# Attention scores and dilated value products of two heads issued in turn into halves of the array, with the dilated mask added on VectorE

## The chip, the cores and the metric

The kernel runs on one core of one Trainium2 chip. The metric is the device time of one execution in microseconds (us), the median of several runs; lower is better.

## The reference

A two-layer encoder on 256 tokens of width 1024, in float32. Each layer is a sandwich-normed mixer and a gated MLP with a centred convolution. The mixer projects the normed input once and splits the result into gates and three kinds of attention:

```python
proj = jnp.einsum('bsd,dc->bsc', h, w_in[l])
gates, mla_in, dil_in, diff_in = jnp.split(proj, SPLITS, axis=-1)
o_mla = mla_mixer(...)        # 8 heads, keys 64 + 32 wide, values 64 wide
o_dil = dilated_mixer(...)    # 6 heads of 64, three groups: dilation 1, 4 and 16
o_diff = diff_mixer(...)      # 4 heads, each softmax(q0 k0) - lam * softmax(q1 k1), 64 wide; values 128 wide
merged = g_mla * (o_mla @ w_branch_mla[l]) + g_dil * (o_dil @ w_branch_dil[l]) + g_diff * (o_diff @ w_branch_diff[l])
x = x + rms_norm(merged @ w_out[l], attn_post_norm[l])
x = x + rms_norm(conv_gated_mlp(rms_norm(x, ...), w_up[l], ffn_conv[l], w_down[l]), ffn_post_norm[l])
```

In the dilated mixer, a query sees the keys of its own residue class that lie within a radius. The three groups' outputs are weighted by the softmax of their log-sum-exps, which is the same as one softmax over the scores of the three groups side by side.

## The kernel before, in words

Weights stream in 87 **pieces** a layer (`PIECES`, line 72). SyncE loads a piece into one of three buffers, ScalarE copies it to a rounded high part `w_hi` (line 617), VectorE subtracts to get the low part `w_lo` (line 906), and TensorE does three matmuls for each product (low by high, high by low, high by high: lines 1170 to 1172). A piece of four 512-column blocks is 24 such matmuls (two row tiles, four blocks, three passes).

The order of all engines is one hand-made list of steps (`plan_steps`, line 116), which each engine walks through in its own program. Step `w` uses a piece: TensorE multiplies it, while ScalarE and VectorE prepare the piece two further on. The attention steps lie between the `w` steps:

- `score i` (28 a layer): i 0 to 7 is latent attention, one query tile of two heads (contraction over 96 rows, line 1337). i 8 to 15 is differential attention, one of the two softmaxes of a head (contraction over 64 rows, either rows 0 to 63 or 64 to 127, line 1343). i 16 to 27 is dilated attention, one query tile of one head: a bf16 matmul of an identity by the mask (line 1348) writes the mask into the bank, then one product of 256 columns and two of 128 are added to it (lines 1349 and 1351; contraction over 64 rows). Odd and even i have their own PSUM banks (4 and 5) and their own slot of `probs`.
- The softmax of score i: VectorE takes the negated maximum (lines 931 and 934), ScalarE the exponential with its sum (lines 791 and 795), VectorE scales (lines 946 to 961).
- `tp i`: TensorE transposes the 128 by 512 probabilities in four parts (line 1416) into bank 6, the only one for it after the first ten; ScalarE copies them to `probsT` (lines 681 and 684), which has two slots. For i 8, 10, 12, 14 there is none.
- `pv g` (14 a layer): value products into bank 7. g 0 to 3 is a pair of latent heads, each into its own 64 output partitions (line 1367), head after head; g 4 to 7 is a differential head over the full array (line 1373); g 8 to 13 is one dilated head into 64 output partitions (lines 1380 and 1383). ScalarE and VectorE empty the bank (lines 803 to 805 and 967 to 975).
- `tq s`: transposes of queries and keys staged by ScalarE and turned by GpSimd's rotation (lines 1406 and 1409), into bank 6 as well; ScalarE empties. `td`: transposes of the differential outputs (line 1423).

A float32 product stands in the trace as two MATMUL records. A transpose is one record.

The order before, in the stretch of the dilated scores, is `score i, pv, w, tp i-1, score i+1, w, tp i, ...`: one `w` between two scores.

Of the kernel before, what the change touches and what calls it, by code (L numbers as in the profile page):

```python
# [16 lines left out]
P = 128  # L39
# [11 lines left out]
HD = 64  # L51
# [63 lines left out]

def plan_steps():
# [163 lines left out]
def build_trunk(nc, a, out):  # L280
    with ExitStack() as ctx:
# [15 lines left out]
        ident_b = sb("ident_b", [P, P], BF16)  # L297
# [9 lines left out]
        half = sb("half", [P, 1])  # L307
        head_squares = sb("head_squares", [P, SEQ])
# [4 lines left out]
        with ExitStack() as one:  # L313
# [13 lines left out]
            probsT = sb("probsT", [P, 2, 4, SEQ], scope=one)  # L327
# [37 lines left out]


# [120 lines left out]
        def _(pool):  # L487
# [11 lines left out]
            for h in range(2):  # L499
# [4 lines left out]
            nc.gpsimd.memset(ident_b[:], 0.0)  # L504
            nc.gpsimd.memset(mask[:], 0.0)
            pool.drain()
            nc.gpsimd.affine_select(out=ident_b[:], in_=ident_b[:], compare_op=ALU.not_equal, fill=1.0, base=0,
                                    pattern=[[-1, P]], channel_multiplier=1)
# [89 lines left out]
        def _(act):  # L598
# [55 lines left out]
            def empty_t(l, key):  # L654
# [20 lines left out]
                elif what == "tp":  # L675
                    g, qt = i // 2, i % 2
                    if g >= 2:

                        act.wait_ge(o_full, l * 14 + (g - 1))
                    if 8 <= i < 16:  # L680
                        nc.scalar.activation(probsT[:, g % 2, 0:2, :].rearrange("p k (t q) -> p t k q", t=2),
                                             T_BANK[:].rearrange("p (t k q) -> p t k q", t=2, k=2), ACT.Copy).then_inc(t_emptied, 1)
                    else:
                        nc.scalar.activation(probsT[:, g % 2, :, qt * P:qt * P + P], T_BANK[:].rearrange("p (b q) -> p b q", b=4),  # L684
                                             ACT.Copy).then_inc(t_emptied, 1)
# [59 lines left out]
            with act.Fori(0, DEPTH) as l:  # L745
                split_hi(l, 0)
                for step in STEPS:
# [31 lines left out]
                    elif what == "score":  # L779
                        i = step[1]  # L780
                        act.wait_ge(max_done, l * 28 + (i + 1))
                        if 10 <= i <= 16 and i % 2 == 0:

                            act.wait_ge(probs_ready, l * 28 + i)
                        elif i >= 2:

                            act.wait_ge(t_full, l * NTB + (T_OF[("tp", i - 2)] + 1))
                        b = i % 2
                        if i < 16:
                            for h in range(2):  # L790
                                last = nc.scalar.activation(probs[:, b, h * SEQ:(h + 1) * SEQ], S_BANK[b][:, h * SEQ:(h + 1) * SEQ], ACT.Exp,
                                                            bias=negmax[:, 2 * b + h:2 * b + h + 1],
                                                            accum_out=rowsum[:, 2 * b + h:2 * b + h + 1])
                        else:
                            last = nc.scalar.activation(probs[:, b, :], S_BANK[b][:], ACT.Exp, bias=negmax[:, 2 * b:2 * b + 1],
                                                        accum_out=rowsum[:, 2 * b:2 * b + 1])
                        last.then_inc(exp_done, 1)
                    elif what == "pv":
                        g = step[1]
                        if g < 4 or g >= 8:  # L800
                            act.wait_ge(o_full, l * 14 + (g + 1))
                            if g < 4:
                                nc.scalar.activation(mla_oT[:, g, 0, :], O_BANK[:, 0:SEQ], ACT.Copy).then_inc(o_hi, 1)
                            elif g % 2 == 1:
                                nc.scalar.activation(dil_oT[:, (g - 8) // 2, 0, :], O_BANK[:, 0:SEQ], ACT.Copy).then_inc(o_hi, 1)
# [36 lines left out]
        def _(dve):  # L842
# [84 lines left out]
            def negmax_of(l, i):  # L927
                b = i % 2
                dve.wait_ge(score_full, l * 28 + (i + 1))
                if i < 16:  # L930
                    V.tensor_reduce(negmax[:, 2 * b:2 * b + 2], S_BANK[b][:].rearrange("p (h k) -> p h k", h=2), AX.X, ALU.max,
                                    negate=True).then_inc(max_done, 1)
                else:
                    V.tensor_reduce(negmax[:, 2 * b:2 * b + 1], S_BANK[b][:], AX.X, ALU.max, negate=True).then_inc(max_done, 1)
# [29 lines left out]
            def empty_o(l, g):  # L964
# [3 lines left out]
                elif g < 8:  # L968
                    dve.wait_ge(o_full, l * 14 + (g + 1))
                    h = g - 4  # L970
                    V.tensor_copy(diff_o[:, :, h * P:(h + 1) * P], O_BANK[:, 0:SEQ].rearrange("p (t d) -> p t d", t=2)).then_inc(o_emptied, 1)
                elif g % 2 == 1:
                    pair = (g - 8) // 2
# [74 lines left out]
            with dve.Fori(0, DEPTH) as l:  # L1048
# [5 lines left out]
                for step in STEPS:  # L1054
# [40 lines left out]
                    elif what == "score":  # L1095
                        negmax_of(l, step[1])
                        normalise(l, step[1])
# [48 lines left out]
        def _(pe):  # L1146
# [54 lines left out]
            def use_piece(l, n):  # L1201
# [30 lines left out]
                if kind == "bmla" or kind == "bdil":  # L1232

                    pe.wait_ge(o_emptied, BASE + l * 11 + (4 if kind == "bmla" else 11))
# [30 lines left out]
            def turn(l, what):  # L1265
# [9 lines left out]
                if what == "merged":  # L1275
                    pe.wait_ge(o_emptied, BASE + l * 11 + 11)
# [49 lines left out]
            def scores(l, i):  # L1326
                if i in (0, 4, 8, 16):
                    wait_heads(l, i)
                b = S_BANK[i % 2]
                qt = i % 2  # L1330
                q = slice(qt * P, qt * P + P)
                if i >= 2:
                    pe.wait_ge(exp_done, l * 28 + (i - 1))
                if i < 8:
                    pair = i // 2
                    for h in range(2):
                        last = PE.matmul(b[:, h * SEQ:(h + 1) * SEQ], mla_qT[0:QK_M, 2 * pair + h, q], mla_kT[0:QK_M, 2 * pair + h, :], start=True, stop=True)
                elif i < 16:

                    head, m = i // 2 - 4, i % 2  # L1340
                    r = slice(64 * m, 64 * m + 64)
                    for t in range(NT):
                        last = PE.matmul(b[:, t * SEQ:(t + 1) * SEQ], diff_qT[r, head, t * P:(t + 1) * P], diff_kT[r, head, :], start=True, stop=True)
                else:
                    head = i // 2 - 8
                    pe.wait_ge(masks_ready, 1)
                    r = slice(64 * (head % 2), 64 * (head % 2) + 64)
                    PE.matmul(b[:], ident_b[:], mask[:, qt, :], start=True, stop=False, skip_group_check=True)
                    PE.matmul(b[:, 0:SEQ], dil_qT[r, head // 2, 0, q], dil_kT[r, head // 2, 0, :], start=False, stop=True, skip_group_check=True)
                    for g in (1, 2):  # L1350
                        last = PE.matmul(b[:, P + g * P:2 * P + g * P], dil_qT[r, head // 2, g, q], dil_kT[r, head // 2, g, q],
# [116 lines left out]
```

## Time and profile before

| | |
|---|---|
| median of 3 runs | 1103.39 us (1103.26 to 1105.31) |
| span of the profiled execution | 1100.7 us |
| TensorE busy | 1081.7 us, 98% |
| VectorE, ScalarE, GpSimd busy | 60%, 53%, 11% |
| granted TensorE clock, mean | 0.996 |
| HBM traffic | 154 GB/s over the span |

The span runs from the first to the last instruction of one profiled execution. The page of the profile gives no device time of its own for that execution, so the span is set beside the median of the runs, which is 2.7 us longer. Busy time of TensorE counts each matmul from its start to its modelled end, and matmuls overlap in the pipeline: the pace has to be read from start to start.

### The profile page before, as it was taken

How to read it: one execution, taken by the hardware profiler on the slowest of the kernel's cores; microseconds unless marked ns; L12 is line 12 of the kernel's file. 1: busy time of each engine (PE TensorE's matmuls, PEld its weight loads, DVE VectorE, ACT ScalarE, POOL GpSimd, SP SyncE). 2: the span in 40 equal slices, each digit the busy share in tenths (PEclk: the TensorE clock that was granted, in tenths of full speed). 3: DMA queues.
4: the chain of work that ended last, by engine and by line, in shares of the span. 5: the costliest groups of instructions: out<-in, count | busy, mean ns of one | idle time of the engine just before them, and what ended most of it. 6: DMA issues, size and time to landing. Idle time of an engine off the chain costs nothing.

```text
span 1100.7 us, 18061 instructions
## 1 busy us (share of the span) xinstructions
PE 1081.7 (98%) x6428; PEld 954.0 (87%) x6428; DVE 663.8 (60%) x842; ACT 585.6 (53%) x843; POOL 124.3 (11%) x237
## 2 busy tenths in 40 slices
PE   8999999999999999999999999999999999999997
PEld 8889889877778899999888898898877779999996
DVE  5535556555476777677664455655545767776765
ACT  5556655454435754555476566555544466455552
POOL 3252113100000000000014321221000000000000
PEclk9999999999999999999999999999999999999999
DMA  6654444533344455455355544364333445546541
GB/s 191 217 163 144 118 123 163 177 130 115 134 154 153 134 192 205 164 206 189 117 178 168 155 135 125 115 194 152 115 121 127 155 133 192 200 164 212 189 157 38
DMA packets 105665, 170.98 MB, mean 155 GB/s; under 512 B 3057, under 2 KB 72484, under 8 KB 105572
## 3 DMA queue, kind: packets, MB, share of 16 engines
q1 hardware_dynamic: 104564, 166.37, 46.2%
q10 hardware_dynamic: 864, 3.15, 1.0%
q8 instruction: 54, 0.88, 0.3%
q0 software_dynamic: 144, 0.26, 0.1%
q14 instruction: 39, 0.32, 0.1%
HBM read 168.72 MB, written 1.05 MB: 154 GB/s over the span
## 4 chain that ended last, share of the span: by engine, by line
issue 45%; PE 45%; POOL 3%; POOLq 3%; DVE 2%; ACT 1%; DVEq 1%; DMA 1%; SPq 0%; ACTq 0%
PE bank L1170 14%; PE bank L1172 14%; PE bank L1171 14%; POOLq L546 2%; POOL stage L547 1%; PE bank L1156 1%; POOLq L573 1%; DVE hT_lo L923 1%; POOL rope_b L545 1%; POOL small L590 1%; DMA par_rows<-in_ffn_conv_dram 1%; POOL rope_a L544 0%; POOL stage L548 0%; POOL roots L594 0%; PE bank L1299 0%
## 5 line engine op out<-in xcount | busy, mean ns | idle before, releaser
L906 DVE TENSOR_TENSOR w_lo<-w_raw,w_hi 128x2048 fp32r<-128x2048 f32 (+3 forms) x174 | 361.7, 2091 | 146.8 <-ACT w_hi L617 146.7
L617 ACT ACTIVATE w_hi<-w_raw 128x2048 fp32r<-128x2048 f32 (+3 forms) x174 | 302.7, 1753 | 35.0 <-PE bank L1172 29.1
L1170 PE MATMUL bank<-w_hi,hT_lo 128*128 128x512 f32 (+2 forms) x704 | 260.6, 370 | 1.8 <-DVE hT_lo L923 1.8
L1172 PE MATMUL bank<-w_hi,hT_hi 128*128 128x512 f32 (+2 forms) x704 | 254.4, 361 | 0.0
L1171 PE MATMUL bank<-w_lo,hT_hi 128*128 128x512 f32 (+2 forms) x704 | 253.9, 361 | 0.0
L1170 PE MATMUL bank<-hT_hi,w_lo 128*128 128x256 f32 x704 | 200.0, 284 | 3.4 <-DVE hT_lo L923 3.4
L1171 PE MATMUL bank<-hT_lo,w_hi 128*128 128x256 f32 x704 | 199.1, 283 | 0.0
L1172 PE MATMUL bank<-hT_hi,w_hi 128*128 128x256 f32 x704 | 199.0, 283 | 0.0
L1170 PEld LDWEIGHTS bank<-w_hi,hT_lo 128*128 128x128 f32 x704 | 132.2, 188 | 19.5 <-issue 2.7
L1172 PEld LDWEIGHTS bank<-w_hi,hT_hi 128*128 128x128 f32 x704 | 132.1, 188 | 14.2
L1171 PEld LDWEIGHTS bank<-w_lo,hT_hi 128*128 128x128 f32 x704 | 132.4, 188 | 12.9
L1170 PEld LDWEIGHTS bank<-hT_hi,w_lo 128*128 128x128 f32 x704 | 134.8, 192 | 6.0 <-DVE hT_lo L923 5.1
L1171 PEld LDWEIGHTS bank<-hT_lo,w_hi 128*128 128x128 f32 x704 | 134.9, 192 | 0.8
L1172 PEld LDWEIGHTS bank<-hT_hi,w_hi 128*128 128x128 f32 x704 | 134.9, 192 | 0.0
L822 ACT ACTIVATE conv_out<-bank,par 128x256 f32<-128x256 f32 x88 | 36.9, 471 | 125.5 <-PE bank L1172 125.5
L594 POOL TENSOR_TENSOR roots<-mean_squares,minus_half 128x1 f32<-128x1 f32 x12 | 6.5, 546 | 667.2 <-DVE mean_squares L1004 667.2
L1127 DVE SCALAR_TENSOR_TENSOR conv_out<-bank,par,conv_out 128x255 f32<-128x255 f32 x88 | 38.4, 478 | 54.4 <-ACT conv_out L822 54.4
L1170 PE MATMUL bank<-w_hi,g_lo 128*128 128x512 f32 x176 | 69.6, 396 | 0.8 <-DVE g_lo L1141 0.8
L1172 PE MATMUL bank<-w_hi,g_hi 128*128 128x512 f32 x176 | 69.5, 395 | 0.0
L1171 PE MATMUL bank<-w_lo,g_hi 128*128 128x512 f32 x176 | 69.5, 395 | 0.0
L684 ACT ACTIVATE probsT<-bank 128x512 f32<-128x512 f32 x40 | 23.8, 594 | 66.3 <-PE bank L1416 66.3
L834 ACT ACTIVATE g_hi<-conv_out 128x512 fp32r<-128x512 f32 x22 | 25.0, 1135 | 47.0 <-DVE conv_out L1139 47.0
(200 smaller groups left out, 1341.2 us busy)
## 6 DMA issues: line engine op xcount, KB each, us to landing
w_raw<-in_w_up_dram SPq DMA_DIRECT2D x44, 1024.0 KB, 5.1
w_raw<-in_w_in_dram SPq DMA_DIRECT2D x36, 1024.0 KB, 5.1
w_raw<-in_w_in_dram SPq DMA_DIRECT2D x36, 768.0 KB, 4.4
w_raw<-in_w_down_dram SPq DMA_DIRECT2D x22, 1024.0 KB, 5.4
w_raw<-in_w_out_dram SPq DMA_DIRECT2D x8, 1024.0 KB, 5.0
w_raw<-in_w_in_dram SPq DMA_DIRECT2D x8, 672.0 KB, 5.8
w_raw<-in_w_branch_mla_dram SPq DMA_DIRECT2D x4, 1024.0 KB, 4.8
w_raw<-in_w_branch_diff_dram SPq DMA_DIRECT2D x4, 1024.0 KB, 4.8
```

Of the source, the lines that this page charges most:

```text
L545: nc.gpsimd.tensor_tensor(sa, xr, s, ALU.mult)
L546: pool.drain()
L547: nc.gpsimd.tensor_tensor(xr[:, :, 0, :], ca[:, :, 0, :], sa[:, :, 1, :], ALU.subtract)
L617: nc.scalar.activation(w_hi[:, n % RING, 0:nk * cols], raw[:, n % RING, 0:nk * cols], ACT.Copy).then_inc(hi_done, 1)
L684: nc.scalar.activation(probsT[:, g % 2, :, qt * P:qt * P + P], T_BANK[:].rearrange("p (b q) -> p b q", b=4), ACT.Copy).then_inc(t_emptied, 1)
L822: last = nc.scalar.activation(conv[:, u % 2, b, j * SEQ:(j + 1) * SEQ], bank[4 + c % 4][:, j * SEQ:(j + 1) * SEQ], ACT.Copy, scale=par[:, ...
L834: nc.scalar.activation(by_class2(g_hi[:, u % 2, :]), own_order2(conv[:, u % 2, 1, :]), ACT.Copy).then_inc(g_hi_done, 1)
L906: V.tensor_tensor(w_lo[:, n % RING, s], raw[:, n % RING, s], w_hi[:, n % RING, s].bitcast(F32), ALU.subtract).then_inc(lo_done, 1)
L1127: V.scalar_tensor_tensor(out=cv[:, o + 1:o + SEQ], in0=src[:, o:o + SEQ - 1], scalar=par[:, ch:ch + 1], in1=cv[:, o + 1:o + SEQ], op0=ALU. ...
L1170: PE.matmul(dst, lhs[1], rhs_hi, start=start, stop=False)
L1171: PE.matmul(dst, lhs[0], rhs_lo, start=False, stop=False)
L1172: return PE.matmul(dst, lhs[0], rhs_hi, start=False, stop=stop)
```

## The change

The 28 score steps become 14 pairs. The four score matmuls of a differential head are issued in turn into rows 0 to 63 and 64 to 127 of the array, each half into its own bank; likewise the six of two dilated heads on one query tile. The dilated value products of two heads are issued together, in turn into output partitions 0 to 63 and 64 to 127 (6 steps become 3), and the latent ones take the two heads in turn. The mask matmul and its identity go; VectorE adds the mask while it takes the maximum, and writes the negated sum to `probs`, from which ScalarE takes the exponential. A score pair waits for the previous pair's maxima (dilated) or exponentials (the others). `probsT` has four slots in place of two. A pair has two `w` steps after it; the second transpose of the previous pair stands behind the score.

```diff
+PAIRS = 14
+NPV = 11
+LAST_PAIR = [0, 1, 2, 3, 4, 5, 6, 7, 9, 11, 13]
 def plan_steps():
...
-    for i in range(28):
-        s.append(("score", i))
-        if i >= 3 and i % 2 == 1:
-            s.append(("pv", (i - 2) // 2))
-        for _ in range(4 if i == 15 else 1):
-            turn_staged(1)
-            if i in (21, 22):
-                s.append(("td", i - 21))
-            w()
-        if i == 19:
-            s.append(("heads",))
-        if i >= 1 and i - 1 not in (8, 10, 12, 14):
-            s.append(("tp", i - 1))
-    w()
+    for p in range(PAIRS):
+        products = [g for g in range(NPV) if LAST_PAIR[g] + 2 == p]
+        if products:
+            turn_staged(1)
+            s.append(("pv", products[0]))
+        turned = [i for i in (2 * p - 2, 2 * p - 1) if p and i not in (8, 10, 12, 14)]
+        s += [("tp", i) for i in turned[:1]]
+        s.append(("score", p))
+        s += [("tp", i) for i in turned[1:]]
+        s.append(("soft", p))
+        w()
+        s.append(("norm", p))
+        for _ in range(3 if p == 7 else 1):
+            if p in (10, 11):
+                s.append(("td", p - 10))
+            turn_staged(1)
+            w()
+        if p == 9:
+            s.append(("heads",))
+    s.append(("tp", 26))
+    w()
     s.append(("tp", 27))
     w()
-    s.append(("pv", 13))
+    s.append(("pv", 10))
...
-            probsT = sb("probsT", [P, 2, 4, SEQ], scope=one)
+            probsT = sb("probsT", [P, 4, 4, SEQ], scope=one)
...
+            def negmax_of(l, p):
+                if p >= 8:
+                    dve.wait_ge(score_full, l * 28 + (2 * p + 2))
+                    dve.wait_ge(t_full, l * NTB + (T_OF[("tp", 2 * p - 1)] + 1))
+                    if p == 8:
+                        dve.wait_ge(masks_ready, 1)
+                    V.memset(wait_slot[:], 0.0)
...
+                        V.tensor_tensor_reduce(out=probs[:, b, :], in0=S_BANK[b][:], in1=mask[:, qt, :], scale=-1.0, scalar=3.0e38,
+                                               op0=ALU.add, op1=ALU.min, accum_out=negmax[:, 2 * b:2 * b + 1]).then_inc(max_done, 1)
...
+            def scores(l, p):
+                if p > 8:
+                    pe.wait_ge(max_done, l * 28 + 2 * p)
+                elif p:
+                    pe.wait_ge(exp_done, l * 28 + 2 * p)
...
+                elif p < 8:
+                    head = p - 4
                     for t in range(NT):
+                        for m in range(2):
+                            r = slice(64 * m, 64 * m + 64)
+                            last = PE.matmul(S_BANK[m][:, t * SEQ:(t + 1) * SEQ], diff_qT[r, head, t * P:(t + 1) * P], diff_kT[r, head, :],
+                                             start=True, stop=True)
...
+                    pair, qt = dil_place(2 * p)[0:2]
+                    q = slice(qt * P, qt * P + P)
+                    for g in range(DIL_G):
+                        cols = slice(0, SEQ) if g == 0 else slice(P + g * P, 2 * P + g * P)
+                        for h in range(2):
+                            r = slice(64 * h, 64 * h + 64)
+                            last = PE.matmul(S_BANK[h][:, cols], dil_qT[r, pair, g, q], dil_kT[r, pair, g, :] if g == 0 else dil_kT[r, pair, g, q],
+                                             start=True, stop=True)
...
-                    PE.matmul(b[:], ident_b[:], mask[:, qt, :], start=True, stop=False, skip_group_check=True)
...
+                    pair = g - 8
                     for kt in range(2):
+                        for h in range(2):
+                            vs = slice((2 * pair + h) * HD, (2 * pair + h) * HD + HD)
+                            PE.matmul(O_BANK[64 * h:64 * h + 64, 0:SEQ], v_dil[:, kt, 0, vs], probsT[:, probs_slot(g, h), kt, :],
+                                      start=kt == 0, stop=False, skip_group_check=True)
                     for dg in (1, 2):
                         for t in range(NT):
+                            for h in range(2):
+                                vs = slice((2 * pair + h) * HD, (2 * pair + h) * HD + HD)
+                                last = PE.matmul(O_BANK[64 * h:64 * h + 64, t * P:t * P + P], v_dil[:, t, dg, vs],
+                                                 probsT[:, probs_slot(g, h), 1 + dg, t * P:t * P + P],
+                                                 start=False, stop=dg == 2, skip_group_check=True)
```

## Rows read from the trace of the kernel before

**Rows 1.** The page, part 1: busy time, share of the span and instructions of each engine

```profile
PE 1081.7 (98%) x6428; PEld 954.0 (87%) x6428; DVE 663.8 (60%) x842; ACT 585.6 (53%) x843; POOL 124.3 (11%) x237
```

**Rows 2.** TensorE's longest wait in total: us, times, longest

```profile
PE bank L1170 <- DVE hT_lo L923: 5.2, 9, 1.8
```

**Rows 3.** A stretch of dilated attention: length, busy PE, PEld, DVE, ACT, POOL, clock, DMA share, GB/s

```profile
190.00:270.00 80.00, 80.00 (x404) 64.71 (x403) 40.48 (x45) 38.76 (x51) 5.70 (x2) 1.00 0.46 151
```

**Rows 4.** TensorE in order of time, last latent score record and a differential score: start, us

```profile
104.18 0.38 PE L1337 MATMUL bank<-mla_kT,mla_qT 96*128 96x256 f32 x1
...
136.04 0.27 PE L1416 MATMUL bank<-ident,probs 128*128 128x128 f32 x1
136.24 1.13 PE L1343 MATMUL bank<-diff_kT,diff_qT 64*128 64x256 f32 x4
...
137.58 0.34 PE L1171 MATMUL bank<-w_lo,hT_hi 128*128 128x384 f32 x1
137.75 0.34 PE L1172 MATMUL bank<-w_hi,hT_hi 128*128 128x384 f32 x1
```

**Rows 5.** TensorE in order of time around a dilated score and product

```profile
224.06 0.60 PE L1416 MATMUL bank<-ident,probs 128*128 128x128 f32 x4
224.50 0.38 PE L1348 MATMUL bank<-mask,ident_b 128*128 128x512 bf16 x1
224.81 0.70 PE L1349 MATMUL bank<-dil_kT,dil_qT 64*128 64x256 f32 x2
225.34 0.60 PE L1351 MATMUL bank<-dil_kT,dil_qT 64*128 64x128 f32 x4
225.88 1.08 PE L1380 MATMUL bank<-probsT,v_dil 128*64 128x256 f32 x4
226.79 1.04 PE L1383 MATMUL bank<-probsT,v_dil 128*64 128x128 f32 x8
227.76 0.50 PE L1170 MATMUL bank<-w_hi,hT_lo 128*128 128x512 f32 x1
228.09 0.39 PE L1171 MATMUL bank<-w_lo,hT_hi 128*128 128x512 f32 x1
228.32 0.40 PE L1172 MATMUL bank<-w_hi,hT_hi 128*128 128x512 f32 x1
```

**Rows 6.** TensorE in order of time around a latent product

```profile
104.49 1.09 PE L1367 MATMUL bank<-probsT,v_mla 128*64 128x256 f32 x8
105.51 0.55 PE L1409 MATMUL bank<-ident,stage 128*128 128x128 f32 x3
```

**Rows 7.** Groups of matmuls by form, whole span: count, busy us, mean ns of one

```profile
L1343 PE MATMUL bank<-diff_kT,diff_qT 64*128 64x256 f32 x64 | 18.0, 402 | 0.0
L1383 PE MATMUL bank<-probsT,v_dil 128*64 128x128 f32 x96 | 12.4, 273 | 0.0
...
L1161 PE MATMUL bank<-ident,par_rows 44*128 44x44 f32 x6 | 0.6, 236 | 1.5 <-DMA par_rows<-in_ffn_conv_dram 1.5
```

**Rows 8.** Transposes of the parameters at the start, in order of time

```profile
9.55 0.56 PE L1161 MATMUL bank<-ident,par_rows 44*128 44x44 f32 x6 [1.52 <-DMA par_rows<-in_ffn_conv_dram]
```

**Rows 9.** All engines in order of time, a dilated score's transposes and softmax

```profile
236.68 1.91 ACT L617 ACTIVATE w_hi<-w_raw 128x2048 fp32r<-128x2048 f32 x1
238.48 0.68 ACT L651 ACTIVATE gates<-bank,small 128x512 f32<-128x512 f32 x1
238.62 2.29 DVE L906 TENSOR_TENSOR w_lo<-w_raw,w_hi 128x2048 fp32r<-128x2048 f32 x1 [1.08 <-ACT w_hi L617]
240.74 0.60 PE L1416 MATMUL bank<-ident,probs 128*128 128x128 f32 x4
241.53 0.59 ACT L684 ACTIVATE probsT<-bank 128x512 f32<-128x512 f32 x1
...
242.66 0.69 DVE L934 TENSOR_REDUCE small<-bank 128x1 f32<-128x512 f32 x1 [1.76 <-PE bank L1351]
243.39 0.69 ACT L795 ACTIVATE probs<-bank,small 128x512 f32<-128x512 f32 x1 [1.27 <-DVE small L934]
```

More of the change, by code:

```diff
@@ L364, in t_bank, with dil_place, probs_slot @@
             return bank[6 + n % 2] if n < N_EARLY else bank[6]
+        def dil_place(i):
+            k = i - 16
+            return k // 4, k % 4 // 2, k % 2
+        def probs_slot(g, part):
+            return g % 4 if g < 8 else 2 * (g % 2) + part
         ss = small[:, 0:8]
@@ L778, in _ @@
                         empty_t(l, step)
[L779 to L797, printed above, removed]
@@ new lines, in _ @@
+                    elif what == "soft":
+                        p = step[1]
+                        for i in (2 * p, 2 * p + 1):
+                            b = i % 2
+                            act.wait_ge(max_done, l * 28 + (i + 1))
+                            if i >= 16:
+                                last = nc.scalar.activation(probs[:, b, :], probs[:, b, :], ACT.Exp, bias=negmax[:, 2 * b:2 * b + 1], scale=-1.0,
+                                                            accum_out=rowsum[:, 2 * b:2 * b + 1])
+                            else:
+                                if i >= 10 and b == 0:
+                                    act.wait_ge(probs_ready, l * 28 + i)
+                                elif i >= 2:
+                                    act.wait_ge(t_full, l * NTB + (T_OF[("tp", i - 2)] + 1))
+                                for h in range(2):
+                                    last = nc.scalar.activation(probs[:, b, h * SEQ:(h + 1) * SEQ], S_BANK[b][:, h * SEQ:(h + 1) * SEQ], ACT.Exp,
+                                                                bias=negmax[:, 2 * b + h:2 * b + h + 1],
+                                                                accum_out=rowsum[:, 2 * b + h:2 * b + h + 1])
+                            last.then_inc(exp_done, 1)
@@ L1094, in _ @@
                         last.then_inc(lat_normed, 1)
-                    elif what == "score":
+                    elif what == "soft":
                         negmax_of(l, step[1])
-                        normalise(l, step[1])
+                    elif what == "norm":
+                        normalise(l, 2 * step[1])
+                        normalise(l, 2 * step[1] + 1)
                     elif what == "pv":
@@ L1324, in wait_heads @@
                 pe.wait_ge(t_emptied, BASE + l * NTB + (last + 1))
[L1326 to L1341, printed above, removed]
-                    for t in range(NT):
-                        last = PE.matmul(b[:, t * SEQ:(t + 1) * SEQ], diff_qT[r, head, t * P:(t + 1) * P], diff_kT[r, head, :], start=True, stop=True)
-                else:
-                    head = i // 2 - 8
-                    pe.wait_ge(masks_ready, 1)
-                    r = slice(64 * (head % 2), 64 * (head % 2) + 64)
-                    PE.matmul(b[:], ident_b[:], mask[:, qt, :], start=True, stop=False, skip_group_check=True)
-                    PE.matmul(b[:, 0:SEQ], dil_qT[r, head // 2, 0, q], dil_kT[r, head // 2, 0, :], start=False, stop=True, skip_group_check=True)
-                    for g in (1, 2):
-                        last = PE.matmul(b[:, P + g * P:2 * P + g * P], dil_qT[r, head // 2, g, q], dil_kT[r, head // 2, g, q],
-                                         start=False, stop=True, skip_group_check=True)
-                last.then_inc(score_full, 1)
@@ L1364, in products @@
                 if g < 4:
-                    for h in range(2):
-                        for kt in range(2):
+                    pt = probsT[:, probs_slot(g, 0), :, :]
+                    for kt in range(2):
+                        for h in range(2):
                             last = PE.matmul(O_BANK[64 * h:64 * h + 64, 0:SEQ], v_mla[:, kt, 2 * g + h, :], pt[:, 2 * h + kt, :],
```

82 lines of the change are left out of this document (47 added, 35 removed).

## The prediction

> **What bounds the kernel now.** I read the page first: TensorE is busy 98% of the span, VectorE 60%, ScalarE 53% [rows 1]. Then TensorE's waits: the largest sum for one producer is 5.2 us in nine waits, at the turns between stages, not in attention [rows 2]. Then a stretch of dilated attention: TensorE has no idle time in 80 us, at full clock (1.00 of 2.4 GHz), while VectorE works 40.5 and ScalarE 38.8 us and the DMA engines are busy 46% [rows 3]. So in the attention part the end is set by the sum of TensorE's issue steps. What is taken from those steps comes off the time one for one, until something else is late. Matmuls overlap in the pipeline, so their durations (0.38 us for 256 columns) are not their price; the distance from start to start is.
>
> **Unit prices, from start to start.** A float32 product is two records. Four records of 256 columns last 1.13 us from the first start to the last end, and one lasts 0.38 [rows 4]: three steps in 0.75. The first is stretched by 0.10, part of a change of division (below), which leaves 0.216 a step. Eight records of 128 columns take 1.04, one lasts 0.27 [rows 5]: seven steps in 0.77, 0.109 each.
>
> A change of how the array is divided also costs. The transpose at 136.04 has its step of 0.109, so the score could start at 136.15. The next full-array matmul whose distance is regular is at 137.58; less its predecessor's step (137.75 less 137.58, about 0.17) the array was free again at 137.40 [rows 4]. The score took 1.25 us, of which four steps are 0.86. The remaining 0.39 is two changes, 0.19 each. From half rows straight to half columns is cheaper: 0.54 from 225.34 to 225.88, less four steps of 0.109, plus 0.05 that the first product's step is too long, so 0.15 [rows 5].
>
> Check of the units on a dilated score with its product: mask 0.22, change 0.19, scores 2 x 0.216 + 4 x 0.109 = 0.87, change 0.15, products 4 x 0.216 + 8 x 0.109 = 1.74, change 0.19: 3.36. Measured: from 224.50 to 228.09 less one step of 0.23 (228.32 less 228.09), 3.36 [rows 5].
>
> **Do halves run at the same time?** For column halves the trace answers. The latent product has eight records of 256 columns, four for each half of the output partitions, and all of them fit between 104.49 and 105.51, 1.02 us [rows 6]. One after the other they would take 8 x 0.216 = 1.73; four steps are 0.86. So two halves overlap fully, though the code issues one head's four records and then the other's. The dilated product of before has one head and pays every step (0.91 us for four records of 256, rows 5). For row halves no row of before shows two at once: the nearest is this one. The bounds are full overlap and none. I take full overlap, since nearest is the column case, and here each half has its own source partitions and its own bank.
>
> **The change, part by part, per layer.**
> - *Differential scores.* Before 8 steps of 1.25 [64 records in two layers, rows 7], one of them directly beside a latent product, which saves 0.19: 9.8. After 4 pairs. With full overlap a pair costs what one cost, 1.25: 5.0. Saved 4.8.
> - *Dilated scores and products.* Before 12 scores and 6 products [96 product records of 128 columns, rows 7], five products directly behind a score: 5 x 3.36, seven lone scores of 0.22 + 0.19 + 0.87 + 0.19 = 1.47, one lone product of 0.19 + 1.74 + 0.19 = 2.1: 29.2. After 6 pairs of 1.25 (no mask) and 3 products of 2.1: 13.8. Saved 15.4. In it the mask is 12 x 0.22 = 2.6, the changes of division some 3, the overlap the rest.
> - *Latent products.* Already overlapped [rows 6]. Nothing. If the new order of issue broke the overlap, it would cost 0.86 each (see the last rival).
> - *Steps that overlap need a faster issue.* Where 128-column records of two halves alternate, a record must start each 0.055 us. The fastest full-array sequence shown is six transposes of 44 columns in 0.56 us [rows 8], less one's 0.24 [rows 7]: 0.065 a step. At that pace a dilated product's 16 short records take 1.04 in place of 0.87, and a score pair's eight 0.52 in place of 0.44. Bounds: nothing, or (3 x 0.17 + 6 x 0.08) x 2 = 2.0 us in all. I take 1.
> - *Mask on VectorE.* A tensor-tensor with accumulation replaces a reduction of 0.69 [rows 9]. Not shown before; the nearest rows are that reduction and the 2048-column subtraction of 2.29, which is 0.57 for 512 columns [rows 9]; doubled it would be 1.4. Twelve a layer: from -1 to +8 us of VectorE a layer, which stands idle half the time here [rows 3]. Cost nothing. What hides it are the two pieces behind each score, 24 steps of 0.23 each, 11 us. The chain inside them: two maxima 1.4, two exponentials with their sum reads under 2, `w_hi` 1.91, `w_lo` 2.29, two scalings shorter than the exponentials, some 9 us if nothing overlaps [rows 9]. If it were longer than the cover, the next pair's first transpose would be late. The memset and the exponential's reading from `probs` are of the same kind: hidden.
> - *Waits.* The second transpose of a pair now stands right behind the score, and bank 6 has to be emptied in between. Transposes at 240.74, last end at 241.34, copy from 241.53 to 242.12: 1.38 after the start [rows 9]. TensorE comes back after 0.44 + 1.25 = 1.69. That just fits if ScalarE is free; a gate tile of 0.68 or a `w_hi` of 1.91 in front would not [rows 9]. There are 9 such places a layer, and 6 where a staged transpose stands ahead of the product and the first transpose in the same bank. 30 places: bounds 0 and about 1 us each. I take 0.1, since the tile copy in front is the one just released and mostly done: 3 us.
> - *GpSimd and SyncE.* Two short set-up instructions less on GpSimd, long before anything waits for them; SyncE's loads keep their order. Nothing. The stretch needs a 1 MB piece every 7 us in place of 8, at 46% DMA.
>
> **Sum.** Two layers: -(4.8 + 15.4) x 2 = -40.4; +1 +3: -36.4. The profiled span is 1100.7; the median of the runs is 2.7 above it, and I carry that over: 1103.4 - 36.4 = 1067.0.
>
> One rule speaks against the size. The Trainium skill, "TensorE: Matmul & The Clock Gate", section on LDWEIGHTS, prices a weight load at its number of columns over 1.2 GHz, which I work out as 107 ns for 128 columns. If loads into two row halves queued, a dilated pair's 12 loads would take 1.28 us in place of 0.87, and the sum would be some 5 us less, an estimate by that page, 1072. The transposes 0.065 us apart, each with its own 128-column load, do not agree [rows 8].
>
> **Rivals.**
> 1. *Row halves do not overlap* (the change does half of what it says). Then a differential pair costs 8 x 0.216 + 0.39 = 2.12, a dilated one 2 x 0.87 + 0.38 = 2.12. Saved per layer: 9.8 - 8.5 = 1.3, and 29.2 - (12.7 + 6.3) = 10.2. In all 23; with the 4 of waits and issue, 1084. For it: no row shows it, and both halves write all 128 partitions of PSUM. Against: rows 6. The Trainium skill, "TensorE: Matmul & The Clock Gate", part 3, says that matmuls in distinct row groups run at once and gives a measured 3.07 times for four; "TensorEngine Tiling (Array Packing)", Gotcha 1, asks for different PSUM banks, which the pairs have. No run so far shows either.
> 2. *Waits in bank 6 or in the softmax chain.* The 30 places at 0.5 us instead of 0.1: 15 in place of 3: 1079. For it: ScalarE takes tiles, copies and exponentials strictly in order, and in differential attention it also has the copies of staged transposes. Against: 1.38 against 1.69, and ScalarE free half the time [rows 3].
> 3. *Slower: each change of half drains the array, as a change of division does.* The new orders alternate at every product: 3 alternations in each of 8 differential pairs, 5 in 12 dilated pairs, 3 in 8 latent products, 11 in 6 dilated products: 174. A drain also ends every overlap: no gain on rows (+17.4 against the forecast), 8 x 0.86 = 6.9 on the latent products, 6 x 1.74 = 10.4 on the dilated ones. Without the drain's own price that leaves 1067 + 34.7 = 1101.7; it passes 1103.4 from 10 ns a change, and at 0.19 us it is 1101.7 + 33 = 1135. For it: the 0.19 is real. Against: with rows 6 the halves interleave in time without one.
>
> **How the numbers follow.** About 0.2% (2.2 us) is what a measurement of this kernel can tell. Forecast 1067 (from 1060 with no waits and no issue cost or a little more gain than counted, to 1073 with issue-bound or queued loads): 0.70. Rival 1, 1084: 0.12. Rival 2, around 1079: 0.14. Rival 3: 0.04, of which 0.03 is slower and 0.01 within 0.2%. The range 1060 to 1086 takes in the first three.
>
> **What would show it.** Lines of the differential and dilated scores: the groups of two halves should start within 0.02 us of each other, and a pair's block from the last full-array step to the next should be 1.25 us (2.1 if rival 1). Dilated products: one block of 2.1 for two heads. TensorE's waits: a new row with bank 6, transposes <- ScalarE `probsT` or staged copies, some 3 us in all (15 if rival 2), most of it visible as issue gaps ahead of the transposes. TensorE still near 98% busy; no VectorE or ScalarE row ahead of the score. The MLP part from line 822 on must keep its length. I am wrong if the attention stretches of both layers together shrink by less than 31 us or more than 43.

## The result, and the profile after

The changed kernel takes 1059.37 us (median of 4, 1059.21 to 1059.49) against 1104.04 for the kernel before (median of 4, 1103.26 to 1105.31). The ratio is 0.9596, 95% interval 0.9584 to 0.9608: 44.7 us, 4.0% faster. The forecast was 1067.0 with a range of 1060 to 1086. Direction and mechanism held; the time lies 0.6 us below the range.

The page of the changed kernel, part 1, beside [rows 1]:

```profile
PE 1036.8 (98%) x6404; PEld 931.1 (88%) x6404; DVE 657.6 (62%) x878; ACT 588.8 (56%) x843; POOL 123.0 (12%) x235
```

TensorE is still busy 98% of a span that is 43.0 us shorter (1057.7). Of its 6428 records only the 24 for the mask are gone, yet its busy time is 44.9 us less: most of that is records that now lie over each other. The groups by form show that best, beside [rows 7]:

```profile
L1363 PE MATMUL bank<-diff_kT,diff_qT 64*128 64x256 f32 x64 | 9.1, 402 | 0.0
L1375 PE MATMUL bank<-dil_kT,dil_qT 64*128 64x256 f32 x48 | 8.4, 428 | 0.0
L1411 PE MATMUL bank<-probsT,v_dil 128*64 128x128 f32 x96 | 6.3, 273 | 0.0
```

Count and mean are those of before (64 at 402 ns, 96 at 273 ns), but the busy time, which counts overlapping records once, is half: 18.0 became 9.1, 12.4 became 6.3.

TensorE in order of time around a dilated product and a score pair of the changed kernel, beside [rows 5]:

```profile
231.16 0.39 PE L1189 MATMUL bank<-w_hi,hT_hi 128*128 128x512 f32 x1
231.48 1.08 PE L1405 MATMUL bank<-probsT,v_dil 128*64 128x256 f32 x8
232.39 1.04 PE L1411 MATMUL bank<-probsT,v_dil 128*64 128x128 f32 x16
233.37 0.66 PE L1445 MATMUL bank<-ident,probs 128*128 128x128 f32 x4
233.95 1.15 PE L1375 MATMUL bank<-dil_kT,dil_qT 64*128 64x256 f32 x12
235.03 0.66 PE L1445 MATMUL bank<-ident,probs 128*128 128x128 f32 x4
235.44 0.48 PE L1187 MATMUL bank<-w_hi,hT_lo 128*128 128x512 f32 x1
```

Eight records of line 1405 last the 1.08 us that four took before, sixteen of line 1411 the 1.04 that eight took. A score pair of twelve records takes 1.15 from first start to last end. The second transpose follows the score at 235.03 with no idle time.

ScalarE and VectorE of the same pair, beside [rows 9]:

```profile
234.14 0.60 ACT L686 ACTIVATE probsT<-bank 128x512 f32<-128x512 f32 x1 [0.27 <-PE bank L1445]
...
235.73 0.69 DVE L948 CUSTOM_DVE_ANT_0 probs<-bank,mask 128x512 f32<-128x512 f32 x1 [1.41 <-PE bank L1375]
...
236.34 0.08 DVE L948 DVE_READ_ACCUMULATOR2_ANT small<- 128x1 f32 x1
...
242.90 0.49 DVE L976 TENSOR_SCALAR probs<-probs,small 128x512 f32<-128x512 f32 x1
...
246.91 0.60 PE L1445 MATMUL bank<-ident,probs 128*128 128x128 f32 x4
```

The mask with its maximum costs 0.69 and 0.08 us, hardly more than the reduction of before. The scaled probabilities are ready at 243.39, the first transpose comes at 246.91: 3.5 us to spare. The copy out of bank 6 ends at 234.74, the second transpose comes at 235.03: 0.3 to spare, as worked out. TensorE's waits (idle time in us, number of waits, the longest) name neither bank 6 nor the softmax; the largest are:

```profile
PE bank L1187 <- DVE hT_lo L927: 5.5, 9, 2.1
PE bank L1178 <- DMA par_rows<-in_ffn_conv_dram: 2.2, 1, 2.2
PE bank L1316 <- DVE merged L1059: 1.9, 2, 0.9
```

For the experiments one more measure is used, the **attention stretch**: from the first latent score to the first transpose of `merged`, in the trace of the profiled execution. It is 242.6 us in each layer before and 221.0 in each layer after, equal to 0.1 in both layers of every run. A difference "in all" below is twice that of one layer, taken from the unrounded times. The time as a whole is less steady: the first weight matmul begins anywhere from 20.3 to 24.0 us after the start of the span, and the granted clock differs between executions (last section).

### The profile page after: what moved, and what is told of

The parts are those of the page before. It is cut to its first block, busy times and chain, and to the rows that moved or that the text cites. A ratio compares the mean times of both kernels' runs of the same rounds, so it can differ in the third digit from the quotient of the medians.

```text
span 1057.7 us, 17974 instructions
## 1 busy us (share of the span) xinstructions
PE 1036.8 (98%) x6404; PEld 931.1 (88%) x6404; DVE 657.6 (62%) x878; ACT 588.8 (56%) x843; POOL 123.0 (12%) x235
## 4 chain that ended last, share of the span: by engine, by line
PE 47%; issue 43%; POOL 4%; POOLq 3%; DVE 1%; ACT 1%; DMA 1%; DVEq 0%; SPq 0%; ACTq 0%
PE bank L1187 15%; PE bank L1188 15%; PE bank L1189 15%; POOLq L541 2%; POOL stage L542 2%; PE bank L1173 1%; POOLq L568 1%; DVE hT_lo L927 1%; POOL rope_b L540 1%; DMA par_rows<-in_ffn_conv_dram 1%; POOL rope_a L539 0%; POOL roots L589 0%; PE bank L1316 0%; PE bank L1438 0%; PE bank L1435 0%
## 5 line engine op out<-in xcount | busy, mean ns | idle before, releaser
L1187 PEld LDWEIGHTS bank<-w_hi,hT_lo 128*128 128x128 f32 x704 | 132.8, 189 | 17.5 <-DVE hT_lo L927 2.3
L539 POOL TENSOR_TENSOR rope_a<-stage,cosT 128x96 f32<-128x96 f32 (+1 forms) x40 | 27.2, 679 | 167.5 <-ACT stage L631 136.0
```

What stands on the lines that cost most here:

```text
L539: nc.gpsimd.tensor_tensor(ca, xr, c, ALU.mult)
L1187: PE.matmul(dst, lhs[1], rhs_hi, start=start, stop=False)
```

## The experiments

**Row halves: is it overlap?**

```diff
-                            r = slice(64 * m, 64 * m + 64)      # differential
+                            r = slice(0, 64)
...
-                            r = slice(64 * h, 64 * h + 64)      # dilated
+                            r = slice(0, 64)
```

> The changed kernel with both heads (or both softmaxes) of a score pair taken from rows 0 to 63, so the second head's scores are computed from the first head's data and order, count and size of the matmuls stay. Theory A (the gain of the scores is the overlap of row halves): every step is paid singly, 8 differential pairs x 4 x 0.216 + 12 dilated pairs x 0.87 = +17.3 us, 1059.4 to 1076.7, and a dilated pair's block goes from 1.23 to 2.10. Theory B (the gain came from fewer changes of division and from the mask, the halves only look simultaneous in the records): no change, 1059.

1077.14 us (ratio to before 0.9758, 0.9742 to 0.9774), stretch 229.8: +8.7 a layer, 17.5 in all, against 17.3 expected. TensorE of this run in order of time, around one dilated pair:

```profile
195.79 0.65 PE L1445 MATMUL bank<-ident,probs 128*128 128x128 f32 x4
196.37 2.02 PE L1375 MATMUL bank<-dil_kT,dil_qT 64*128 64x256 f32 x12
198.32 0.50 PE L1187 MATMUL bank<-w_hi,hT_lo 128*128 128x512 f32 x1
```

The same twelve records take 2.02 in place of 1.15. The rival falls: the two row halves work at once, at full pace each, and that is worth 17.5 us.

**Column halves.**

```diff
-                            PE.matmul(O_BANK[64 * h:64 * h + 64, 0:SEQ], v_dil[:, kt, 0, vs], ...
+                            PE.matmul(O_BANK[0:64, SEQ * h:SEQ * h + SEQ], v_dil[:, kt, 0, vs], ...
...
-                                last = PE.matmul(O_BANK[64 * h:64 * h + 64, t * P:t * P + P], v_dil[:, t, dg, vs],
+                                last = PE.matmul(O_BANK[0:64, SEQ * h + t * P:SEQ * h + t * P + P], v_dil[:, t, dg, vs],
```

> The changed kernel with the dilated products of both heads written to output partitions 0 to 63 (the second head's to the other half of the bank's columns), so partitions 64 to 127 are left as they were. Number, order and size of the matmuls stay. Theory A (half columns overlap in the pair): 6 products x 1.74 = +10.4 us, 1069.8; the product's block 2.04 to 3.8. Theory B: no change.

1068.99 us (0.9680, 0.9664 to 0.9696), stretch 226.2: +5.2 a layer, 10.3 in all, as expected. TensorE of this run in order of time, at a dilated product for two heads:

```profile
232.53 1.94 PE L1405 MATMUL bank<-probsT,v_dil 128*64 128x256 f32 x8
234.30 1.91 PE L1411 MATMUL bank<-probsT,v_dil 128*64 128x128 f32 x16
236.14 0.66 PE L1445 MATMUL bank<-ident,probs 128*128 128x128 f32 x4
```

**The mask, from both sides.**

```diff
+                    for h in range(2):
+                        PE.matmul(S_BANK[h][:], ident_b[:], mask[:, qt, :], start=True, stop=False, skip_group_check=True)
...
-                        V.tensor_tensor_reduce(out=probs[:, b, :], in0=S_BANK[b][:], in1=mask[:, qt, :], ...
+                        V.tensor_reduce(negmax[:, 2 * b:2 * b + 1], S_BANK[b][:], AX.X, ALU.max, negate=True)
```

> The changed kernel with the mask put back on TensorE: a bf16 identity times mask into each bank ahead of the pair's scores, the maximum and the exponential read from PSUM as in the kernel before. Theory A (TensorE's steps set the time): 24 steps of 0.21 to 0.26 us, +5.1 to +6.2 us, to about 1065. Theory B (the mask was hidden behind something else, or the pairing is worth less with it): under +2 us.

1063.6 us (0.9636, 0.9619 to 0.9652), stretch 223.7: +5.3 in all, where 24 mask steps of 0.216 are 5.2. TensorE of this run in order of time, with two of them ahead of a score:

```profile
190.47 0.59 PE L1369 MATMUL bank<-mask,ident_b 128*128 128x512 bf16 x2
191.00 1.15 PE L1374 MATMUL bank<-dil_kT,dil_qT 64*128 64x256 f32 x12
```

The other side, the kernel before with the mask moved:

```diff
+        wait_slot = sb("wait_slot", [P, 1])
...
-                    PE.matmul(b[:], ident_b[:], mask[:, qt, :], start=True, stop=False, skip_group_check=True)
...
+                    dve.wait_ge(t_full, l * NTB + (T_OF[("tp", i - 2)] + 1))
+                    V.memset(wait_slot[:], 0.0)
...
+                    V.tensor_tensor_reduce(out=probs[:, b, :], in0=S_BANK[b][:], in1=mask[:, i % 2, :], ...
```

> The kernel before with this one part of the change: the mask added on VectorE, the mask matmul gone; no pairs. Theory A: 24 steps of 0.26 us less, -6.2 us, 1104.0 to 1097.8, if the second softmax wait (VectorE now waits for the transpose two scores back) hides. Theory B (that wait shows, since there is only one piece of weights between scores): between -6 and +3 us.

1094.39 us (0.9909, 0.9893 to 0.9926): 9.5 faster, more than either theory had. The stretch is 6.9 shorter in all. The dilated blocks give only their 0.216 each, 5.2; neither the mask nor a wait explains the rest. Looked at step by step, something else had changed: the branch products' 512-column steps went from 0.233 to 0.228 us, and so had the changed kernel's. Hence the last pair of experiments.

**Placement in SBUF.** The one thing that these kernels share and the kernel before lacks is `wait_slot`, one float per partition, reserved ahead of the large buffers.

```diff
 half = sb("half", [P, 1])
+wait_slot = sb("wait_slot", [P, 1])      # the kernel before, nothing else; not used
```

> The kernel before with one float per partition more reserved in SBUF after half (the changed kernel's wait_slot, here used by nothing), so that every buffer allocated behind it moves. Open is why the branch products' 512-column steps (stationary operand mla_oT, diff_oT, dil_oT) are 0.233 us apart before and 0.227 to 0.228 in the changed kernel and in the one with the mask on VectorE. Theory A (placement of the buffers): the steps fall to 0.228, the attention stretch from 242.6 to 241.8 a layer, 1.6 us of the time. Theory B (something the mask's move does, such as less pressure on the banks from TensorE): steps stay at 0.233 and the stretch at 242.6.

1100.36 us against 1104.10 in the same session (0.9962, 0.9948 to 0.9976): 3.7 us from one unused float. The stretch falls to 241.9. With the mask's 5.2 that makes 8.9 of the 9.5 us of the last experiment. And the changed kernel without it:

```diff
-wait_slot = sb("wait_slot", [P, 1])
+wait_slot = small[:, 60:61]
```

> The changed kernel with wait_slot taken from an unused column of the buffer small, so that the buffers behind it move back by its size (the identity's 256 bytes stay gone). Theory A (placement): the branch products' steps rise from 0.228 to 0.233 and the stretch from 221.0 to 221.8 a layer, 1061.0. Theory B: nothing changes, 1059.4 and 221.0.

1061.97 us (0.9621, 0.9608 to 0.9634), stretch 221.8: 2.6 slower than the changed kernel (measured in an earlier session). Below are the groups by form of the MLP's down products, whose operands `g_hi` and `g_lo` lie behind the spare float: first the kernel before with it, then the changed kernel without.

```profile
L1171 PE MATMUL bank<-w_hi,g_lo 128*128 128x512 f32 x176 | 68.9, 391 | 1.0 <-DVE g_lo L1142 1.0
L1172 PE MATMUL bank<-w_lo,g_hi 128*128 128x512 f32 x176 | 68.7, 391 | 0.0
L1173 PE MATMUL bank<-w_hi,g_hi 128*128 128x512 f32 x176 | 68.5, 389 | 0.0
```

```profile
L1187 PE MATMUL bank<-w_hi,g_lo 128*128 128x512 f32 x176 | 69.6, 396 | 0.8 <-DVE g_lo L1158 0.8
L1188 PE MATMUL bank<-w_lo,g_hi 128*128 128x512 f32 x176 | 69.5, 395 | 0.0
L1189 PE MATMUL bank<-w_hi,g_hi 128*128 128x512 f32 x176 | 69.5, 395 | 0.0
```

Five to six ns of duration, and as much of pace: start to start, 0.2278 against 0.2332 us for these 528 matmuls and for the 264 of the branches, in both kernels the same way. 792 steps by 5.4 ns are 4.3 us. Some of it goes into longer waits for `merged` and `g_lo`: in the changed kernel they are 1.9 and 1.1 us, without the float 1.1 and 0.8. The identity's 256 bytes do nothing: the mask version has them again, and its steps stay at 0.228. Which property of the address does it was not tried.

**Does the order of issue matter?** First half by half.

```diff
-                        for h in range(2):        # inside the loop over the products
+                    for h in range(2):            # outside of it
```

> The changed kernel with the matmuls of a pair issued one half after the other (all of head 0, then all of head 1) in the differential and dilated scores and in the dilated products. Theory A (a half runs ahead of what was issued before it for the other half, as the latent products of the kernel before did): no change, 1059.4, blocks as before and the two halves' records within 0.02 us. Theory B (the alternating order is what makes the halves overlap; latent products are a short case of 8 records): scores lose up to 17.3 us and dilated products up to 10.4 us, up to 1087; if only the long product of 24 records loses it, 1065 to 1070.

1075.42 us (0.9732, 0.9715 to 0.9748), 16 slower; stretch 228.3, 14.6 longer in all. So theory A falls as it was put, and theory B in part. The differential pairs, four records a half, lost nothing (blocks of 1.27 against 1.26). The dilated ones lost much: a score pair takes 1.76 in place of 1.23, a product 3.39 in place of 2.04. TensorE of this run in order of time, at one product of 24 records:

```profile
234.93 1.08 PE L1405 MATMUL bank<-probsT,v_dil 128*64 128x256 f32 x4
235.84 0.71 PE L1410 MATMUL bank<-probsT,v_dil 128*64 128x128 f32 x5
236.28 0.43 PE L1405 MATMUL bank<-probsT,v_dil 128*64 128x256 f32 x1
236.39 0.38 PE L1410 MATMUL bank<-probsT,v_dil 128*64 128x128 f32 x2
236.55 0.38 PE L1405 MATMUL bank<-probsT,v_dil 128*64 128x256 f32 x1
236.61 0.27 PE L1410 MATMUL bank<-probsT,v_dil 128*64 128x128 f32 x1
236.77 0.59 PE L1405 MATMUL bank<-probsT,v_dil 128*64 128x256 f32 x2
237.20 1.04 PE L1410 MATMUL bank<-probsT,v_dil 128*64 128x128 f32 x8
```

Each head has 4 records of line 1405 and 8 of line 1410. The second head's first one (236.28) begins beside the first head's ninth, and three of the first head's records (two at 236.39, one at 236.61) start after it. In the dilated score (six records a half) the second head's first record starts 6 ns after the third, again with three to come. In these blocks a later issued half starts ahead of three records issued before it, and not of more. The test of that reading:

```diff
+                    for h, g in ((0, 0), (0, 1), (1, 0), (1, 1), (0, 2), (1, 2)):
...
-                            for h in range(2):    # products: inner loop
+                        for h in range(2):        # products: around two of one head
```

> The changed kernel with the dilated scores and products issued two products of one head (four records), then two of the other, and so on. Theory A (a half can start while up to four records issued before it for the other half have not started, as the half-by-half run shows: there the second half began four records before the first one's end): full overlap, blocks 1.23 to 1.25 and 2.04 to 2.06, 1059.4 within 1 us. Theory B (only strict alternation, or one head's run of at most four records in the whole block, overlaps): scores up to +10 us, products up to +10 us, 1065 to 1080.

1059.86 us (0.9599, 0.9584 to 0.9614), stretch 221.2. Runs of four records overlap fully (blocks 1.235 and 2.086 against 1.230 and 2.035). Strict alternation isn't needed, short runs are: four records overlap, six (the score of the half-by-half version) do not, five were not tried. The Trainium skill, "TensorE: Matmul & The Clock Gate", part 3, says of matmuls: "strict FIFO, no reordering", and that their starts follow the order of issue. The rows above disagree: records of one half start ahead of earlier issued records of the other.

**How deep is VectorE's cover?**

```diff
+                        for j in range(n):       # n = 1, then 4
+                            V.tensor_reduce(spare[:, k + j:k + j + 1], S_BANK[b][:], AX.X, ALU.max)
                         V.tensor_tensor_reduce(out=probs[:, b, :], ...
```

> The changed kernel with one reduction of 0.69 us over the bank more on VectorE ahead of each dilated maximum (24 in all, 16.6 us of VectorE; its result is used by nothing). The trace of the changed kernel has the scaled probabilities ready at 243.39 and the first transpose of them at 246.91: 3.5 us to spare; one more costs 1.4 a pair. Theory A (VectorE is covered by the two pieces of weights): no change, within 1 us of 1059.4. Theory B (the chain from score to transpose is near the path): +5 to +17 us.

1061.29 us (0.9615, 0.9599 to 0.9631; runs from 1057.6 to 1062.5), stretch 221.3, 0.5 in all longer. Covered. The median is still 1.9 slower, 0.9 more than theory A allowed. In the trace the down products' steps are 0.229 with this kernel's larger spare buffer, which is some 0.7 us. And the four executions differ with their mean granted clock: 1057.6 us at 0.999, 1062.5 at 0.993, 1062.4 at 0.992; those of the changed kernel have 0.994 to 0.996.

> The same with four reductions more a score: 5.5 us a pair, 2 us beyond the 3.5 to spare where no product stands ahead of the transpose. Theory A: the cover ends here, +1.5 to +2.5 us on about 10 of 12 pairs (less where a product gives 2 us more), so +12 to +25 us, 1071 to 1084, with TensorE's waits naming the scaling on VectorE or w_lo. Theory B (there is far more cover than the trace shows): no change.

1075.84 us (0.9747, 0.9731 to 0.9764), stretch 228.8: 15.5 longer in all. The cover ends where the 3.5 us said, and the wait is where rival 2 had put it. From TensorE's waits of this run (idle time in us, number of waits, the longest):

```profile
PE bank L1449 <- DVE probs L980: 9.9, 6, 3.0
```

Not all of the 15.5 is that wait. 1.5 us behind the wait of 3.0 us (218.8 to 221.7) the granted clock falls from 2.4 to 1.2 GHz. The stretch at that clock: length, busy PE, PEld, DVE, ACT, POOL, clock, DMA share, GB/s:

```profile
223.20:226.60 3.40, 3.40 (x16) 2.69 (x13) 3.40 (x6) 0.60 (x1) 0.00 (x0) 0.50 0.94 311
```

Steps of 512 columns take 0.43 there, and TensorE falls back by 1.6 us against the version with one reduction more. The second layer has the same (748.9 to 752.3), so 3.2 of the 15.5 are the clock.

**Fewer changes of division?** Products directly behind a score.

```diff
+            if p not in (5, 11, 13):
                 s.append(("pv", products[0]))
...
         s.append(("score", p))
+        if p in (5, 11, 13):
+            s.append(("pv", products[0]))
```

> The changed kernel with three products a layer (the latent one of pair 5, the dilated ones of pairs 11 and 13) directly behind the score of half rows instead of ahead of the first transpose. Theory A (a change of division costs 0.19 to or from the full array and 0.15 between halves): 6 times about 0.2 us less, 1058.2, blocks of score and product together 3.07 (dilated) in place of 1.23 + 2.04 = 3.27. Theory B (the first transpose, now earlier, waits for its bank or the second for the product's bank): no gain, or up to 2 us more.

1061.94 us (0.9616, 0.9600 to 0.9632), stretch 221.7: 1.3 longer in all. The blocks did shrink (score and dilated product 3.12 together), but in pair 5 the product had covered the copy of a staged transpose out of bank 6. All engines of this run in order of time, at pair 5:

```profile
148.26 0.49 PE L1441 MATMUL bank<-ident,stage 128*128 128x128 f32 x3
148.46 0.58 ACT L634 ACTIVATE stage<-bank,small 128x384 f32<-128x384 f32 x1 [1.50 <-PE bank L1192]
148.94 0.48 ACT L671 ACTIVATE dil_qT<-bank 128x384 f32<-128x384 f32 x1
...
149.55 0.32 PE L1448 MATMUL bank<-ident,probs 128*128 128x128 f32 x1 [0.80 <-ACT dil_qT L671]
```

The tile copy (line 634) stands in front, as the prediction had feared of such places. With `p in (11, 13)` only:

> The changed kernel with only the two dilated products of pairs 11 and 13 behind the score, where no staged transpose stands in front of bank 6; the latent product of pair 5 stays ahead as a cover. Theory A (the loss of the last version was the 0.8 us wait for the copy of the staged transpose): that wait is gone, 4 blocks of 3.12 instead of 1.23 + 2.04 = 3.27, the attention stretch 220.7 in place of 221.0 a layer and the time 0.6 us less than 1059.4, which the median can hardly tell. Theory B (the moved product makes another wait): the stretch stays at 221.0 or grows towards 221.7.

1060.38 us (0.9601, 0.9588 to 0.9614), stretch 220.8: the wait is gone and 0.4 us of stretch won, which the whole time does not show. No version beat the changed kernel beyond what can be measured.

## Why the prediction was right or wrong

Two steps of the prediction failed. Its sum had +3 us for waits and +1 for issue, and the trace shows none of either. And it put the move of the SBUF buffers at nothing, where it is worth 2.6 us. The mechanism and the other terms held; term by term:

**What bounds it**: right. TensorE's steps set the end before and after; what was taken from them came off the time.

**Overlap of row halves**: right. It was taken from the column halves without a row of its own, and the first experiment gives 17.5 us for it against 17.3 by the unit steps.

**Unit prices**: right within 1 us. From the traces, blocks measured from the last full-array step to the next: a differential pair 1.26 (1.25 predicted), a dilated pair 1.23 (1.25), a dilated product for two heads 2.04 (2.1). All blocks of scores and products together went from 109.4 to 68.0 us, 41.4 less; the sum had 40.4. By the experiments it splits into 17.5 for row halves, 10.3 for column halves and 5.3 for the mask. No run isolates the remaining 8.3. They are put down to the changes of division that fell away: 20 a layer by the two step lists, 40 at about 0.2. The prediction's own prices (0.19, and 0.15 between halves) give 7.1 for them.

**Weight loads**: twelve loads and matmuls fit in 0.87 us of steps, and 1072 is far off. With the price that the prediction took from the Trainium skill ("TensorE: Matmul & The Clock Gate", section on LDWEIGHTS, 107 ns for 128 columns), twelve loads one behind the other would take 1.28 us. So the trace does not agree with such a queue.

**Issue of short records, +1**: wrong, it cost nothing. Sixteen 128-column records of two halves take what eight did (1.04), 0.055 us apart on average. The pace of 0.065 in [rows 8] was no bound for halves. Its records are not full-array either, as the prediction has them: they use 44 of the 128 rows.

**Waits, +3**: wrong, they were nil. The 0.3 us to spare between the two transposes, worked out from the rows, was there; the 0.1 for each of 30 places was put on top of a sum that already said "just fits". The version with products behind the score shows that such waits are real (0.8 us where the cover is taken away), so the term belonged in the range and not in the sum.

**Placement, the step that is missing**: `wait_slot` was costed as an instruction ("hidden") and not as a buffer that moves all the others. It is worth 2.6 us in the changed kernel. Without it the kernel takes 1061.97, inside the range.

**The carry from span to median, 2.7**: 1.7 after. The one profile of before was among its shortest executions: its span is 1100.7, and those of its later executions are 1100.5 to 1102.8.

**The 7.6 between 1067.0 and 1059.4** are 1.0 of carry and 6.7 of span (1064.3 forecast, 1057.7 measured). In the traces the span's part is 4.0 (waits and issue that were not there), 1.0 (the blocks gave 41.4 in place of 40.4) and 4.3 (placement). Against it stand 0.9 of longer waits behind the faster steps, 1.4 of a fall of the granted clock (last section) and 0.5 of a later first weight matmul. That makes 6.5.

**The range** failed at its lower end. The prediction gave 1060 for "no waits and no issue cost or a little more gain than counted". Without waits and issue its sum is 1063.0. So 3 us were left for gains that no term had, and placement and carry are 3.6.

**Its signs of being wrong**: two came true. The attention stretches together shrank by 43.1 us, where it allowed 43. And the MLP part did not stay as it was: its 528 down-product steps lost 2.9 us by the placement.

**Rivals**: 1 fell by the first experiment. 2 fell here, and was brought about by hand twice. 3, a drain at each change of half, fell with the first trace: alternating records start 6 to 7 ns apart.

## What to carry to other kernels

Two products with half the contraction rows, or half the output columns, cost one when issued in turn or in runs of at most two float32 products, each half with its own bank or its own output partitions. Where the array is the bound, count start-to-start steps and changes of division (0.19 us here), and let the sum stand without a surcharge for waits that the rows say just fit; the surcharge belongs in the range. When a change adds or drops any SBUF buffer, compare the matmul steps of stages that it does not touch before crediting it with the whole difference.

## What the runs showed of the hardware that was not expected

- One unused float per partition ahead of the large buffers changes the pace of 792 matmuls of 512 columns from 0.233 to 0.228 us and the time by 3.7 us (before) and 2.6 us (after).
- A half's records start ahead of at most three records issued earlier for the other half; a run of twelve leaves the second half idle for the first eight.
- The granted clock falls to 1.2 GHz for a few us in some executions. The second layer's latent pieces (336 columns) have mean steps of 0.171 us in the changed kernel's profile and in four variants' (half by half, runs of two, both with products behind the score), but 0.157 in the others: 1.4 us in all. All five have one such fall there, and no other run has. In the changed kernel it comes right behind a wait of 2.1 us (537.4 to 539.5), and the steps go from 0.280 back to 0.155 when it ends. Two stretches of equal length, at the fall and behind it (length, busy PE, PEld, DVE, ACT, POOL, clock, DMA share, GB/s):

```profile
539.80:543.20 3.40, 3.40 (x14) 3.40 (x14) 3.40 (x7) 3.40 (x7) 0.00 (x0) 0.50 0.78 245
543.20:546.60 3.40, 3.40 (x24) 3.40 (x23) 1.99 (x4) 2.64 (x4) 0.90 (x2) 1.00 0.56 157
```

Runs with as long a wait at that place have no fall (2.1 us without the spare float, 2.3 with one reduction more), so what decides is open.

- The start varies in the same way. Ahead of the first weights, TensorE does 34 transposes of the identity without a pause. They take 3.9 us in the mask version, at full clock, and 6.8 in the kernel before with the spare float, where the clock is at 1.2 GHz from 10.9 to 17.7:

```profile
10.73 3.93 PE L1171 MATMUL bank<-ident 128*128 128x128 f32 x34
11.79 6.80 PE L1157 MATMUL bank<-ident 128*128 128x128 f32 x34
```

The first weight matmul follows at 20.3 in the one and at 24.0 in the other; 2.9 of the 3.7 us are these transposes. A difference of one or two us between two medians can be such falls of the clock, and not the change.
